# A two-layer hybrid decoder trunk: the first opening takes in a fourth weight unit, its low parts go to GpSimd, and x is loaded first

## What is computed

```
h = rmsnorm(x, g_pre) * (1 + scale) + shift        # shift, scale, gate: rows of silu(c) @ w_ada + b_ada
y = swiglu(h): (silu(h @ w_gate) * (h @ w_up)) @ w_out
x = x + 0.5 * gate * rmsnorm(y, g_post)
```

## Time and profile before

| | |
|---|---|
| median of 3 executions | 2716.25 us |
| lowest, highest | 2715.87, 2718.5 us |
| the profiled execution | 2716.15 us |
| its span in the profile | 2714.4 us |
| GpSimd's busy share | 10% |

### The profile page before, as it was taken

One profiled execution on the slowest core, in us unless ns is written; L12 is line 12 of the kernel. 1 busy time (PEld: TensorE's weight loads), 2 busy tenths in 40 slices (PEclk: granted clock), 3 DMA queues, 4 the chain that ended last, 5 costly groups with the idle time before them and its releaser, 6 DMA issues.

```text
span 2714.4 us, 37231 instructions
## 1 busy us (share of the span) xinstructions
PE 2672.1 (98%) x13120; PEld 2159.1 (80%) x13120; DVE 1493.9 (55%) x2525; ACT 1131.6 (42%) x2053; POOL 259.0 (10%) x333
## 2 busy tenths in 40 slices
PE   8999999999999999999999999999999999999999
PEld 6888887677777888888888888877777778888887
DVE  7665445667746556532366563465687375553323
ACT  4322245666545353222252222546665443532222
POOL 0111000112100001110011110002121000011100
PEclk9999999999999999999999999999999999999999
DMA  7555432111222416423245545221112224242232
GB/s 302 206 196 183 155 103 87 63 55 63 78 87 77 116 48 247 175 95 109 86 171 186 196 156 159 89 84 65 63 63 78 86 78 116 94 158 97 100 101 70
DMA packets 94796, 321.83 MB, mean 119 GB/s; under 512 B 16769, under 2 KB 17153, under 8 KB 93378
## 3 DMA queue, kind: packets, MB, share of 16 engines
q1 hardware_dynamic: 94658, 320.07, 34.9%
HBM read 316.72 MB, written 2.13 MB: 117 GB/s over the span
## 4 chain that ended last, share of the span: by engine, by line
PE 87%; DVE 6%; ACT 3%; issue 2%; DVEq 2%; POOL 0%; DMA 0%; ACTq 0%; SPq 0%; POOLq 0%
PE bank L490 20%; PE bank L492 20%; PE bank L491 20%; PE bank L499 7%; PE bank L497 7%; PE bank L498 7%; PE bank L1974 2%; PE bank L1953 2%; DVE w_low L474 1%; PE bank L1944 1%; ACT w_high L468 1%; DVEq L1130 1%; PE bank L1931 1%; DVE scores_sb L1317 1%; PE bank L1844 1%
## 5 line engine op out<-in xcount | busy, mean ns | idle before, releaser
L490 PE MATMUL bank<-h_high,w_high 128*128 128x512 f32 (+1 forms) x2488 | 966.8, 389 | 15.1 <-DVE h_low L1445 13.1
L492 PE MATMUL bank<-h_high,w_low 128*128 128x512 f32 (+1 forms) x2488 | 946.9, 381 | 0.0
L491 PE MATMUL bank<-h_low,w_high 128*128 128x512 f32 (+1 forms) x2488 | 945.6, 380 | 0.0
L474 DVE TENSOR_TENSOR w_low<-w_raw,w_high 128x1024 fp32r<-128x1024 f32 x438 | 565.1, 1291 | 565.6 <-ACT w_high L468 562.4
L468 ACT ACTIVATE w_high<-w_raw 128x1024 fp32r<-128x1024 f32 x438 | 459.2, 1051 | 354.2 <-PE bank L499 313.2
L490 PEld LDWEIGHTS bank<-h_high,w_high 128*128 128x128 f32 x2488 | 470.5, 189 | 114.4 <-issue 25.8
L492 PEld LDWEIGHTS bank<-h_high,w_low 128*128 128x128 f32 x2488 | 469.8, 189 | 90.5
L491 PEld LDWEIGHTS bank<-h_low,w_high 128*128 128x128 f32 x2488 | 470.4, 189 | 83.8 <-issue 1.9
L499 PE MATMUL bank<-w_low,ffn_high 128*128 128x512 f32 x704 | 273.9, 389 | 0.0
L497 PE MATMUL bank<-w_high,ffn_high 128*128 128x512 f32 x704 | 273.9, 389 | 0.0
L498 PE MATMUL bank<-w_high,ffn_low 128*128 128x512 f32 x704 | 273.9, 389 | 0.0
(11 more groups left out here) (221 smaller groups left out, 2591.5 us busy)
## 6 DMA issues: line engine op xcount, KB each, us to landing
w_raw<-stream SPq DMA_DIRECT2D x438, 512.0 KB, 3.6
ada_raw<-ada SPq DMA_DIRECT2D x128, 512.0 KB, 3.6
ada_start<-ada SPq DMA_DIRECT2D x8, 1024.0 KB, 17.9
post_gain<-post_gain_row SPq DMA_DIRECT2D x6, 512.0 KB, 6.3
mixer_consts<-mixc SPq DMA_DIRECT2D x2, 1152.0 KB, 5.2
x<-x_in SPq DMA_DIRECT2D x4, 512.0 KB, 6.6
silu_c<-silu_row SPq DMA_DIRECT2D x4, 512.0 KB, 4.3
out<-x SPq DMA_DIRECT2D x8, 256.0 KB, 2.0
```

The lines of the kernel that those rows point to most:

```text
L474: eng.tensor_tensor(wL[:, slot], raw[:, slot], wH[:, slot].bitcast(F32), ALU.subtract).then_inc(lo_ready[slot].sem, 1)
L490: eng.matmul(o, a, rhs_h, start=first, stop=False)
L491: eng.matmul(o, a, rhs_l, start=False, stop=False)
L492: return eng.matmul(o, b, rhs_h, start=False, stop=last)
```

## The change

Seven edits, all in the first opening:

- SyncE loads the identity first (a semaphore `ident_in` of its own), then x; c's row, the small parameters and c's column come between x's blocks 1 and 2. Unit 3 is loaded behind the second group of w_ada instead of the last.
- ScalarE does the two tanh of c between the squares of x's blocks 1 and 2, and the high part of unit 3 behind row 1 instead of at the end.
- VectorE keeps the lows of units 0 and 1 and of row 0. It no longer does the lows of rows 1 to 7 and of units 2 and 3, and waits for all rows before it leaves the opening.
- GpSimd does, in this order: low of unit 2, of row 1, of unit 3, of rows 2 to 7.
- TensorE waits only for the identity and x's first block; its fills read x instead of c's row, six and two in place of eight and three, and none between the rows.
- `scale_row(1)` stands behind units 0 and 1 of k = 0. Unit 2 runs one row behind units 0 and 1, unit 3 two rows behind.
- The first turn has no unit left.

```diff
@@ sync
+            sp.dma_start(ident[:, :], consts[:, 0:P]).then_inc(ident_in.sem, 16)
             for tb in range(TB):
                 sp.dma_start(x[:, tb], x_in[:, tb]).then_inc(x_loaded[tb].sem, 16)
+                if tb == 1:
+                    sp.dma_start(c_row[:, :], cvec.partition_broadcast(P)).then_inc(consts_in.sem, 16)
+                    sp.dma_start(parv[:, 0:3 * KD], par0).then_inc(consts_in.sem, 16)
+                    sp.dma_start(skt[:, 0:KD], ccol).then_inc(consts_in.sem, 16)
             for g in range(KD):
                 sp.dma_start(ada_start[:, 2 * g:2 * g + 2], ada0[:, 2 * g:2 * g + 2]).then_inc(ada_start_in[g].sem, 16)
-                if g == 0:
-                    for u in range(LEAD):
-                        sp.dma_start(raw[:, u], stream[u]).then_inc(raw_full[u].sem, 16)
-            sp.dma_start(raw[:, LEAD], stream[LEAD]).then_inc(raw_full[LEAD].sem, 16)
+                for u in ((0, 1, 2), (LEAD,))[g] if g < 2 else ():
+                    sp.dma_start(raw[:, u], stream[u]).then_inc(raw_full[u].sem, 16)
@@ gpsimd
+            def start_low(j):
+                pool.wait_ge(start_hh.sem, j + 1)
+                pool.tensor_tensor(hL[:, j], tu[:, j % 2], hH[:, j].bitcast(F32), ALU.subtract
+                                   ).then_inc(start_h.sem, 1)
             pool.wait_ge(start_ms.sem, 1)
             pool.tensor_tensor(rsx, msx, mhalf[:, 0:TB], ALU.pow).then_inc(start_rs.sem, 1)
+            split_low(pool, 0, 2)
+            pool.wait_ge(start_h.sem, 1)
+            start_low(1)
+            split_low(pool, 0, LEAD)
+            for j in range(2, KD):
+                start_low(j)
@@ scalar
             for tb in range(TB):
+                if tb == 2:
+                    s.wait_ge(consts_in.sem, 16 * 3)
+                    s.activation(skt[:, KD:2 * KD], skt[:, 0:KD], ACT.Tanh, scale=0.5).then_inc(c_tanh.sem, 1)
+                    s.activation(silu_start[:, :], c_row[:, :], ACT.Tanh, scale=0.5).then_inc(c_tanh.sem, 1)
...
                 if j == 0:
-                    for u in range(1, LEAD):
-                        split_high(s, 0, u)
-            split_high(s, 0, LEAD)
+                    split_high(s, 0, 1)
+                    split_high(s, 0, 2)
+                elif j == 1:
+                    split_high(s, 0, LEAD)
@@ vector
                 if j == 0:
                     split_low(v, 0, 0)
-                    start_low(0)
-                    for u in range(1, LEAD):
-                        split_low(v, 0, u)
-                elif j >= 2:
-                    start_low(j - 1)
-            start_low(KD - 1)
-            split_low(v, 0, LEAD)
+                    v.wait_ge(start_hh.sem, 1)
+                    v.tensor_tensor(hL[:, 0], tu[:, 0], hH[:, 0].bitcast(F32), ALU.subtract).then_inc(start_h.sem, 1)
+                    split_low(v, 0, 1)
+            v.wait_ge(start_h.sem, KD)
@@ tensor
-            fill(8)
+            pe.wait_ge(x_loaded[0].sem, 16)
+            fill(6)
             pe.wait_ge(silu_col_ready.sem, 1)
             scale_row(0)
             pe.wait_ge(start_xn[0].sem, 2)
             pe.wait_ge(start_xn[1].sem, 2)
             for j in range(4):
                 x_tile(j)
-            fill(3)
+            fill(2)
             for k in range(KD):
-                if k + 1 < PE_ROWS:
-                    scale_row(k + 1)
                 if 4 <= k + 3 < KD:
                     x_tile(k + 3)
                 pe.wait_ge(start_h.sem, k + 1)
+                unit_product(0, k)
+                unit_product(1, k)
                 if k == 0:
+                    scale_row(1)
+                if k >= 1:
+                    unit_product(2, k - 1)
+                if k >= 2:
+                    unit_product(LEAD, k - 2)
-                if PE_ROWS - 1 <= k < KD - 2:
-                    fill(1, 3)
+            unit_product(2, KD - 1)
+            unit_product(LEAD, KD - 2)
+            unit_product(LEAD, KD - 1)
...
-                    turn(0, range(LEAD, 4))
+                    turn(0, range(LEAD if f or l else LEAD + 1, 4))
```

More of the change, by code:

```diff
@@ L347, in trunk_kernel @@
         consts_in = sig("consts_in", 0)
+        ident_in = sig("ident_in", 0)
         x_loaded = [sig(f"x_loaded{i}", 0) for i in range(TB)]
@@ L1014, in shift_col @@
                 return lambda j: mod[:, c * KD + j:c * KD + j + 1]
-            s.wait_ge(consts_in.sem, 16 * 4)
-            s.activation(skt[:, KD:2 * KD], skt[:, 0:KD], ACT.Tanh, scale=0.5).then_inc(c_tanh.sem, 1)
-            s.activation(silu_start[:, :], c_row[:, :], ACT.Tanh, scale=0.5).then_inc(c_tanh.sem, 1)
             for tb in range(TB):
+                if tb == 2:
+                    s.wait_ge(consts_in.sem, 16 * 3)
+                    s.activation(skt[:, KD:2 * KD], skt[:, 0:KD], ACT.Tanh, scale=0.5).then_inc(c_tanh.sem, 1)
+                    s.activation(silu_start[:, :], c_row[:, :], ACT.Tanh, scale=0.5).then_inc(c_tanh.sem, 1)
                 s.wait_ge(x_loaded[tb].sem, 16)
@@ L1498, in _ @@
             b1 = mod_sum
-            v.wait_ge(consts_in.sem, 16 * 4)
+            v.wait_ge(ident_in.sem, 16)
+            v.wait_ge(consts_in.sem, 16 * 3)
             v.tensor_scalar(b1[:, :], parv[:, KD:2 * KD], 1.0, None, ALU.add)
@@ L1515, in _ @@
                                 ).then_inc(start_xn[1].sem, 1)
-            def start_low(j):
-                v.wait_ge(start_hh.sem, j + 1)
-                v.tensor_tensor(hL[:, j], tu[:, j % 2], hH[:, j].bitcast(F32), ALU.subtract).then_inc(start_h.sem, 1)
             for j in range(KD):
@@ L1703, in first_opening, with fill @@
         def first_opening(pe):
-            def fill(count, b=0):
+            def fill(count):
                 for _ in range(count):
-                    pe.matmul(bank[b][:, :], ident[:, :], c_row[:, 0:T], start=True, stop=True)
+                    pe.matmul(bank[0][:, :], ident[:, :], x[:, 0, 0:T], start=True, stop=True)
             def scale_row(j):
@@ L1726, in x_tile, with unit_product @@
                 mm.then_inc(start_tr.sem, 1)
-            fill(8)
+            def unit_product(u, k):
+                if k == 0:
+                    unit_ready(pe, 0, u)
+                mm = product(pe, bank[u][:, :], u, k * P, slice(0, P), hH[:, k], hL[:, k], k == 0, k == KD - 1)
+                if k == KD - 1:
+                    mm.then_inc(unit_done[u].sem, 1)
+            pe.wait_ge(x_loaded[0].sem, 16)
+            fill(6)
             pe.wait_ge(silu_col_ready.sem, 1)
@@ L1733, in first_opening @@
                 x_tile(j)
-            fill(3)
-            slots = None
+            fill(2)
             for k in range(KD):
-                if k + 1 < PE_ROWS:
-                    scale_row(k + 1)
                 if 4 <= k + 3 < KD:
@@ L1741, in first_opening @@
                 pe.wait_ge(start_h.sem, k + 1)
+                unit_product(0, k)
+                unit_product(1, k)
                 if k == 0:
-                    slots = [unit_ready(pe, 0, u) for u in range(LEAD)]
-                for j, slot in enumerate(slots):
-                    mm = product(pe, bank[j][:, :], slot, k * P, slice(0, P), hH[:, k], hL[:, k], k == 0, k == KD - 1)
-                    if k == KD - 1:
-                        mm.then_inc(unit_done[slot].sem, 1)
-                if PE_ROWS - 1 <= k < KD - 2:
-                    fill(1, 3)
+                    scale_row(1)
[6 more added lines that the diff above has]
+            unit_product(LEAD, KD - 1)
         def tensor_mixer(pe, l):
@@ L1982, in _ @@
                 pe.sem_inc(unit_done[slot].sem, 1)
-            pe.wait_ge(consts_in.sem, 16 * 4)
+            pe.wait_ge(ident_in.sem, 16)
             first_opening(pe)
```

4 lines of the change are left out of this document (removed).

## The result

| | before | changed |
|---|---|---|
| median | 2716.90 us (20 executions, 2715.87 to 2719.42) | 2721.49 us (20 executions, 2720.18 to 2724.34) |
| ratio to before, 95% interval | | 1.0017 [1.0011, 1.0023] |
| the profiled execution | 2716.15 us | 2722.12 us |
| its span | 2714.4 us | 2720.3 us |
| unit 4 begun | 53.18 | 56.29 |

The change costs 4.6 us, 0.17%: less than the 0.2% that the prediction took as the bound of what can be told, so by its own terms this is "no change" on the slower side. The interval leaves 1 out. The predicted 2719.0 was 2.5 too low; the range of 2714 to 2723 holds the result. Of the 2.5, 0.7 is the start of the sum: it was added to the profiled execution's 2716.15, and the median of 20 executions of the kernel before is 2716.90. The shift was forecast as 2.7 and is 4.6.

A forecast was written before the change was run, and what follows sets the result against it. TensorE, busy for 98% of the span, was taken as the bound. Unit 4's start shifts 2.84 - 0.4 (start) + 0.3 (clock) = 2.7 us; 2716.15 + 2.7 = 2718.9, given as 2719.0, range 2714 to 2723.

The forecast's parts named there:

- The exclusion: Opening's rows: VectorE's two-input operations and GpSimd's lows exclude each other, holding 1.16 a row; rows 3.51 us apart, against 3.25.
- the chain of the prediction: Opening worked out instant by instant: row 4 at 34.10, row 7 at 44.63, TensorE done at 56.02, 2.84 us later.
- The start: Reordered first loads: 0.4 us gained taken, bounds 0.9 gained and 0.5 lost.
- The order: VectorE against GpSimd: first to ask goes first; unit 3's low enters behind row 3's first dot product.
- The unit's low part: GpSimd's low of 1024 columns in the opening: 2.4 us taken, bounds 1.30 and 2.6.
- Rival 2: TensorE's clock falls before row 0, row 1's scale waits for late sums: 1.8 to 3.5 us more, 2721.7; chance 0.22.
- the main case: Whole kernel: GpSimd's lows hold up VectorE's rows; 2719.0 us, own range 2717.5 to 2721, chance 0.61.
- The clock behind row 1: TensorE's clock falls in the gaps of 24.3 to 28.6 and about 31 to 34.2: cost 0 to 0.6, taken 0.3.
- TensorE's tail: End of the opening: 21 products, 4.77 us, after row 7 is ready, against 33 before.
- After the opening: Unit 4's low ready at 55.4, needed at 56.3, slack 0.9: no stall; at unit 5 up to 1 us.
- a shift there lasts to the end: Behind unit 4's start TensorE goes on at the same pace, so the opening's shift carries through unchanged.

The follow-up runs named there:

- experiment 3: The changed kernel with only the low parts of units 2 and 3 back on VectorE, those of the rows still on GpSimd; 2720.24 us, ratio 1.0013.
- experiment 8: The changed kernel run once more, unaltered, for the spread of its opening; 2722.51 us, ratio 1.0022.
- experiment 4: The kernel before with only the new order of the loads and of ScalarE's two tanh, fills from x; 2717.03 us, ratio 1.0002.
- experiment 1: The changed kernel with all low parts of the opening back on VectorE; 2718.18 us, ratio 1.0004.
- experiment 6: The changed kernel with eight and three fills, and three more each ahead of the products of rows 1 and 2; 2721.81 us, ratio 1.0017.
- experiment 7: From experiment 1: more fills, row 1's sums before row 0's products, unit 2 with each row, fourth unit catching up at rows 6 and 7; 2718.08 us, ratio 1.0004.
- experiment 10: The changed kernel with low parts on VectorE, fills of before, unit 3 loaded behind w_ada's third group, row 1's sums before row 0; 2716.56 us, ratio 0.9999.
- experiment 2: The changed kernel with only the low parts of rows 1 to 7 back on VectorE; 2718.61 us, ratio 1.0006.
- experiment 5: From experiment 3: GpSimd writes zeros by memset for the low parts of rows 1 to 7 instead of subtracting; 2716.07 us, ratio 0.9999.
- the three of 9: The kernel before again (2716.86 us), and with four (2720.36 us) and with two (2719.12 us) more fills behind the last row of h.

## Why the prediction was right, and where not

**The exclusion** was right, and decided the sign. Predicted: rows 3.51 apart; measured 3.56 in the changed kernel and in experiments 3 and 8; 2.65 where GpSimd reads nothing, 2.64 predicted. Row 4 began at 34.12, row 7 at 44.79, and its low part ended at 51.33; the chain of the prediction has 34.10, 44.63 and 51.20, less the 0.4 of the start. The row of 3.56 is 0.05 more than the sum's 3.51 with 1.16, so about 1.21 was held. The Trainium skill ("SBUF — State Buffer", Who interferes with whom) calls the conflict an exclusive lock and says of it, where it speaks of VectorE's two-port modes, that it is kept for the whole instruction; by that a row would be 3.65 with 1.30 in place of 1.16, and the measurement, 3.56, lies between. The prediction called the operation of four columns at 273.05 in the earlier trace rows a subtraction; it is a multiplication, as is the scale of a row, and the reading does not hang on it.

**The order** was right for the first unit, where GpSimd asked 0.15 before the dot product (20.33 against 20.48, a race of 0.07 in the prediction), and wrong for the second. I let the low part of unit 3 in behind row 3's first dot product. It went ahead of it: GpSimd was free at 28.30 and VectorE, held by the scale of row 2, at 28.35. The low part of row 2 then came between the two dot products. Turns were swapped and the sum was the same. That row 4 began at 34.12 where the chain has 34.10 is in part luck: the start gave 0.79, which would make it 33.31, and row 1's late scale took 0.71 of that back.

**The unit's low part** takes 2.37 to 2.46 with at most 0.1 of waiting in it. Taken: 2.4.

**The start**: taken 0.4 gained, measured 0.79 in the profiled execution, and 0.33 as the difference of the means that experiment 4 gives (13.47 and 13.14). Right as a mean; one execution can be 0.5 off.

**Rival 2, the clock before row 0,** was half true. The weight loads of the two fills take 0.33 at 19.29 and 20.14 and 0.19 at 20.91, the sums end late, and row 1's scale waits 0.71 for them. It cost 0.7 of the 2.7 worked out, as the clock was back by 20.9 and the six products of row 0 ran at full rate; in experiment 3 the scale waited 1.7 and in experiment 1 2.5. The prediction made it decide "once the sums are over 1 us late"; by that the profiled execution is the main case, and experiments 1 and 3, with the same TensorE program, are not. And it is not the change's doing alone. I took "before it held" from one execution; the old start shows the same in two of four. A state that one profile shows is no constant of the kernel.

**The clock behind row 1**: predicted to fall there, cost 0 to 0.6, taken 0.3. It fell, and cost nothing that can be seen: TensorE idled 0.53 and 0.54 before rows 5 and 6, and the 0.24 that experiment 6 gained are the 0.26 by which row 1's scale came earlier. The 0.3 in the sum stands where rival 2's 0.7 should, and so the two errors partly cancel. The granted clock does show these falls (0.50 from 28 to 34); only in the first microseconds does it read 1.00 at half rate, as the prediction says.

**TensorE's tail**: 21 products, 4.77 predicted, 4.91 measured. The count holds only at this cadence, as experiments 1 and 7 showed. The prediction did not say that condition. Even in the changed kernel row 6 with its 33 products ends only 0.14 before row 7 with its 21 (48.47 + 7.49 = 55.96, 51.33 + 4.77 = 56.10). Estimates made later missed by it as well: unit 4 came 3.0 behind the expectation in experiment 1 (there with the late row 1) and 3.7 in experiment 7. Moving a quarter of the opening's products forward was worth 0.1 and 0.5 at unit 4 in experiments 7 and 10. The rows were quick there, but row 6 then leaves TensorE 30 to 33 products, as many as row 7 did before, and with unit 3's low part ahead of it row 6 was ready only at 45.0 in experiment 10, where row 7 was ready at 45.11 before.

**After the opening**: unit 4's low part ended 55.68 for 56.29, a slack of 0.6 (0.9 predicted), and no stall there or at unit 5. Unit 4 in all: +3.11 in the profiled execution, +2.87 and +3.37 in experiments 6 and 8, +2.7 in the sum. That step was right to 0.4.

**What failed** is the sentence that "a shift there lasts to the end" and that nothing is added behind. The median rose by 4.6, in experiment 8 by 6.0. Nine profiled executions have the fourth unit in the opening (the changed kernel's, experiments 1, 2, 3, 5, 6, 7, 8 and 10): the shift of the median less that of unit 4 is 1.3 as their mean, from -0.6 to 2.6. For the four others (experiment 4, the three of 9) it is -0.1, from -0.9 to 0.6. The profiles agree, where both ends are of one execution: from unit 4 to the last product 2657.7 as the mean of the nine (2656.0 to 2658.9), 2656.5 of the five with the old end of the opening, the one before among them (2655.4 to 2658.1). The two sets overlap. What the extra time consists of can be seen in the changed kernel at 426, behind 24 single-column matmuls:

```profile
423.50 1.84 PE L1797 MATMUL bank<-ones,squares 128*128 128x1 f32 x16
425.20 1.03 PE L1797 MATMUL bank<-ones,squares_kv 128*128 128x1 f32 x8
426.10 0.49 PE L491 MATMUL bank<-h_high,w_high 128*128 128x512 f32 x1
...
427.22 0.63 PE L492 MATMUL bank<-h_low,w_high 128*128 128x512 f32 x1
427.65 0.63 PE L493 MATMUL bank<-h_high,w_low 128*128 128x512 f32 x1
```

From 427.22 to 430.21 seven products go by, 0.43 apart in place of 0.23. The granted clock of 427 to 430 is 0.50. Such stretches are few: three behind the opening in the profile of before, five in that of after. With these two laid side by side, product by product, the one near 426 puts the changed kernel 1.5 behind and the one near 1002 0.7, as TensorE waits less behind it; together 2.2 of the 2.8 between 2655.7 and 2658.6. Over all fourteen profiles the time goes with their number: with three stretches 2655.4 to 2656.6 (five profiles), with five 2656.9 to 2658.6 (seven). Experiments 2, 3 and 10 have the fourth unit in the opening and only three; the kernel before with fills behind has five. The one near 426 stands in eight of the nine, and in one of the five others, the one with two fills. Why the fourth unit should favour it is not settled, and with so few profiles chance is not excluded. That a shift alone does is not excluded either: the four fills moved the same instructions by more and their median shows nothing added, but its interval is wide. A change in the clock's state at the end of the opening was not tried. The instructions behind unit 4 are the same in both kernels.

So of the 4.6: 3.1 are the opening, and the runs show its parts (rows slower by 0.31 each, the units' low parts in the way, row 1's late scale, less the start and less the 12 products fewer behind row 7). The other 1.5 or so lie behind it, in these two profiles for the most part in slow clock: a difference seen but not explained. Slow clock need not be all of it: over its eleven executions experiment 6 has the mean granted clock of the kernel before (0.9966 and 0.9967), and yet its median rose by 5.3 where unit 4 moved by 2.9. The prediction put it at nothing, with "it goes on like that" as its only reason. That the total still fell into the stated range is owed to the range's width; the main case's own range was too narrow for it.

## What to carry to other kernels

Before work is moved to an idle engine, look for the two engines side by side in the trace: where VectorE has two-input instructions back to back, GpSimd's low parts came out of the same time, 1.2 for a subtraction that VectorE itself does in 0.61, and even a one-column instruction behind them waited 0.9. Work moved ahead of the last row of a pipeline pays only if the rows are the bound at the end; count what the consumer still has to do from the last row but one as well. And when differences of a few us in 2700 matter, take more than one profile of the same kernel: the clock's state in the first 25 us moved unit 4 by 0.9 between executions of the same instructions up to there.

## What the runs showed of the hardware

- The order between the two engines goes by instruction and by some hundredths: at 28.30 against 28.35 GpSimd's subtraction of 2.37 went ahead of a dot product that was already queued, and it did so again in experiments 6 and 8 (28.04 and 28.57). The exclusion takes in the custom dot product and a multiplication of a single column (1.05 to 1.08 in place of 0.16); a memset on GpSimd (0.52) is outside it.
- A GpSimd subtraction of 1024 columns takes 2.37, one of 512 takes 1.29: an estimate from the two is 1.08 for 512 columns and some 0.2 that is fixed.
- TensorE's clock fell with hardly any idle before it: in the two kernels with more fills behind 16 sums and then 16 transposes of 128 columns, with one idle of 0.33 between, and near 426 behind 24 single-column matmuls. In the profile the engine counts as busy there. The same sums and transposes with an idle of 0.34 between ran at the full rate in the second execution of the kernel before (1.97 for the transposes): these instructions allow the fall, they do not fix it.
- The same kernel's executions lie 2.1 to 4.5 us apart (2714.35 to 2718.55 in one set of 33). The spread goes with the clock: in that set the 17 executions with a mean granted clock of 0.996 took 2717.4 on average, the 10 with 0.997 took 2716.0 and the 6 with 0.998 took 2715.5. The profiles of one kernel with four and with three slow stretches differ by 0.6 from unit 4 to the end.
